# Causal mask of an attention stage: VectorE's minimum with a constant tile in the logits' bank, in place of a TensorE product of mask and identity

## The reference, cut to what matters

```python
for i in range(t // Q_BLOCK):
    z = einsum("bhqd,bhkd->bhqk", q_blk, k[:, :, :ctx]) * scale
    mask = k_pos[None, :] < q_pos[:, None]
    log_1m_beta = where(mask, log_sigmoid(-z), 0.0)
    cs = cumsum(log_1m_beta, axis=3)
    log_a = log_sigmoid(z) + (cs[..., -1:] - cs)
    a = where(mask, exp(log_a), 0.0)
    outs.append(einsum("bhqk,bhkd->bhqd", a, v[:, :, :ctx]))
```

```python
gates = sigmoid(z_g.reshape(bsz, t, N_BRANCH, d) + b_gate[l])
merged = gates[:, :, 0] * y_a + gates[:, :, 1] * y_b + gates[:, :, 2] * y_c
```

## Time and profile before

| | us |
|---|---|
| median of 3 runs | 2188.16 |
| lowest and highest | 2187.33, 2188.7 |
| the profiled execution | 2186.91 |
| its span, first to last instruction | 2185.1 |
| TensorE busy in the span | 2152.9 |
| VectorE, ScalarE, GpSimd busy | 1190.1, 914.4, 920.4 |

### The profile page before, as it was taken

The page is one execution under the profiler, slowest core; times in us unless marked ns, Lnnn a source line. Parts: engine busy times, 40 slices in busy tenths (PEclk is TensorE's granted clock), DMA queues, the critical chain, the costliest instruction groups (busy, mean ns, idle before and its releaser), DMA issues.

```text
span 2185.1 us, 25401 instructions
## 1 busy us (share of the span) xinstructions
PE 2152.9 (99%) x9879; PEld 1778.4 (81%) x9879; DVE 1190.1 (54%) x1778; ACT 914.4 (42%) x1329; POOL 920.4 (42%) x438
## 2 busy tenths in 40 slices
PE   8989999999999999999999999999999999999999
PEld 6868888888888888888888888887777788888887
DVE  6874576444346253566763533888566324765351
ACT  5454444333333333345442323534777334443331
POOL 2423444444443343433444444644432454444443
PEclk9999999999999999999999999999999999999999
DMA  3101222323322222222222234322212232233233
GB/s 133 68 20 54 98 94 97 106 87 102 116 87 82 95 84 82 97 72 94 96 97 97 96 97 148 108 86 69 74 62 68 87 131 95 95 98 105 89 105 97
DMA packets 57656, 200.42 MB, mean 92 GB/s; under 512 B 6400, under 2 KB 7168, under 8 KB 57280
## 3 DMA queue, kind: packets, MB, share of 16 engines
q1 hardware_dynamic: 57536, 198.79, 26.9%
HBM read 194.30 MB, written 4.19 MB: 91 GB/s over the span
## 4 chain that ended last, share of the span: by engine, by line
PE 86%; DVE 6%; issue 3%; ACT 3%; POOL 1%; DMA 0%; SPq 0%; DVEq 0%; ACTq 0%; POOLq 0%
PE ps L321 26%; PE ps L323 26%; PE ps L322 26%; DVE ps L2095 3%; PE ps L349 2%; PE ps L350 2%; PE ps L351 2%; ACT WH L292 1%; PE ps L1229 0%; DMA WS<-in_w 0%; PE ps L364 0%; DVE SC L2243 0%; PE ps L1823 0%; DVE SC L2240 0%; ACT SC L2009 0%
## 5 line engine op out<-in xcount | busy, mean ns | idle before, releaser
L302 POOL TENSOR_TENSOR WL<-WS,WH 128x1024 fp32r<-128x1024 f32 (+2 forms) x362 | 855.7, 2365 | 1139.8 <-ACT WH L292 1139.7
L321 PE MATMUL ps<-H,WH 128*128 128x512 f32 (+1 forms) x1776 | 697.2, 393 | 9.2 <-DVE H L534 9.2
L322 PE MATMUL ps<-H,WH 128*128 128x512 f32 (+1 forms) x1776 | 693.3, 390 | 0.0
L323 PE MATMUL ps<-H,WL 128*128 128x512 f32 (+1 forms) x1776 | 693.2, 390 | 0.0
L292 ACT ACTIVATE WH<-WS 128x1024 fp32r<-128x1024 f32 (+2 forms) x362 | 374.7, 1037 | 451.4 <-PE ps L323 348.9
L321 PEld LDWEIGHTS ps<-H,WH 128*128 128x128 f32 (+1 forms) x1776 | 334.1, 188 | 81.9 <-POOL WL L302 7.1
L323 PEld LDWEIGHTS ps<-H,WL 128*128 128x128 f32 (+1 forms) x1776 | 334.0, 188 | 71.2 <-issue 0.6
L322 PEld LDWEIGHTS ps<-H,WH 128*128 128x128 f32 (+1 forms) x1776 | 334.2, 188 | 67.9 <-issue 0.4
L321 PE MATMUL ps<-G,WH 128*128 128x512 f32 x880 | 342.8, 389 | 0.6 <-DVE G L975 0.6
L322 PE MATMUL ps<-G,WH 128*128 128x512 f32 x880 | 342.4, 389 | 0.0
L323 PE MATMUL ps<-G,WL 128*128 128x512 f32 x880 | 342.4, 389 | 0.0
(11 more groups left out here) (259 smaller groups left out, 2014.8 us busy)
## 6 DMA issues: line engine op xcount, KB each, us to landing
WS<-in_w SPq DMA_DIRECT2D x337, 512.0 KB, 3.2
WS<-in_w SPq DMA_DIRECT2D x24, 384.0 KB, 3.0
X<-in_x SPq DMA_DIRECT2D x8, 256.0 KB, 5.4
xs<-X SPq DMA_DIRECT2D x1, 2048.0 KB, 8.2
X<-xs SPq DMA_DIRECT2D x8, 256.0 KB, 5.9
out<-X SPq DMA_DIRECT2D x8, 256.0 KB, 2.9
X<-in_sg SPq DMA_DIRECT2D x1, 1344.0 KB, 5.5
SC<-in_rot SPq DMA_DIRECT2D x4, 256.0 KB, 3.7
```

The source lines that it names most:

```text
L302: e.tensor_tensor(lo, raw, hi.bitcast(F), ALU.subtract).then_inc(*P.sig("w_lo", i))
L321: e.matmul(out, lh, rh, start=start, stop=False)
L322: e.matmul(out, lh, rl, start=False, stop=False)
L323: return e.matmul(out, ll, rh, start=False, stop=stop)
```

## The change

The constant tile `C_STRICT` becomes an upper bound for the logits: 3e38 where the query is after the key, -1e30 elsewhere (`GONE` is -3e38). TensorE no longer adds the mask; its last logits product raises `az`. VectorE waits for `az` and takes the minimum of the first 128 columns of the bank and the constant tile, in place, for each of the 32 items. The absolute values, on ScalarE for even items and on VectorE for odd ones, wait for this minimum. The two tiles of `CR` and their two copies on ScalarE go. `CR` shrinks from 257 columns to one. The semaphore `row_mm` is merged into `spread`.

```diff
-    c[:, C_STRICT:C_STRICT + 128] = np.where(f < p, 0.0, NEG)
+    c[:, C_STRICT:C_STRICT + 128] = np.where(f > p, -GONE, NEG)
...
-    mean = P.m["CR"][:, 256:257].to_broadcast([128, 128])
+    mean = P.m["CR"][:, 0:1].to_broadcast([128, 128])
...
-    e.matmul(b, mean, lo, start=False, stop=True).then_inc(*P.sig("row_mm", name))
+    e.matmul(b, mean, lo, start=False, stop=True).then_inc(*P.sig("spread", (name, "row")))
...
-        for kl, ql in ((0, 0), (0, 1), (1, 0)):
+        for kl, ql in ((0, 0), (0, 1)):
             for z, kk, qq in heads:
-                e.matmul(z, kk[kl], qq[ql], start=kl + ql == 0, stop=False)
-        for hd, (z, _, _) in enumerate(heads):
-            e.matmul(z[:, 0:128], P.m["CR"][:, 128:256], P.m["CR"][:, 0:128], start=False, stop=True).then_inc(
-                *P.sig("az", n + hd))
+                e.matmul(z, kk[kl], qq[ql], start=ql == 0, stop=False)
+        for hd, (z, kk, qq) in enumerate(heads):
+            e.matmul(z, kk[1], qq[0], start=False, stop=True).then_inc(*P.sig("az", n + hd))
...
             if k % 2 == 0:
                 if k >= 2:
                     e.wait_ge(*P.at("v_lo", k - 2))
-                e.wait_ge(*P.at("az", k))
+                e.wait_ge(*P.at("a_mask", k))
                 e.activation(u, P.ps(("az", k))[:, 0:w], ACT.Abs).then_inc(*P.sig("a_abs", k))
...
             z, u = P.ps(("az", k))[:, 0:w], c_soft(P, hd, kt)
+            e.wait_ge(*P.at("az", k))
+            e.tensor_tensor(z[:, 0:128], z[:, 0:128], P.con(C_STRICT), ALU.min).then_inc(*P.sig("a_mask", k))
             if k % 2:
                 if k >= 2:
                     e.wait_ge(*P.at("v_lo", k - 2))
-                e.wait_ge(*P.at("az", k))
+                e.wait_ge(*P.at("a_mask", k))
                 e.tensor_scalar(u.bitcast(I), z.bitcast(I), 0x7fffffff, None, ALU.bitwise_and).then_inc(
                     *P.sig("a_abs_dve", k))
...
-    for o, s in ((0, C_ID), (128, C_STRICT)):
-        e.activation(P.m["CR"][:, o:o + 128], P.con(s), ACT.Copy).then_inc(*P.sig("cr", o))
```

More of the change, by code:

```diff
@@ L422, in act_row @@
     if biased:
-        e.wait_ge(*P.at("row_mm", name))
+        e.wait_ge(*P.at("spread", (name, "row")))
         e.activation(y, P.ps((name, "row")), ACT.Ln, bias=P.con(C_EPS, 1), scale=-2.0).then_inc(*P.sig("row_act", (name, "ln")))
@@ L2388, in act_program @@
     act_dsa(P, e, "nf0")
-    e.activation(P.m["CR"][:, 256:257], P.con(C_MEAN, 1), ACT.Copy).then_inc(*P.sig("cr", "mean"))
+    e.activation(P.m["CR"][:, 0:1], P.con(C_MEAN, 1), ACT.Copy).then_inc(*P.sig("cr", "mean"))
     act_ffn(P, e, 0, "nf0", "nm1", ("feat", ("aout", 7)), [("p_exp", 31)])
@@ L2491, in program @@
                             ("WS", RING * NXW, F), ("X", 8 * T, F), ("SC", 5888, F), ("TMP", 2 * T, F), ("SQ", 2 * T, F),
-                            ("ACC", T, F), ("CR", 257, R), ("PAR", NPAR, F), ("FP", FPN, F), ("CON", NCON, F),
+                            ("ACC", T, F), ("CR", 1, R), ("PAR", NPAR, F), ("FP", FPN, F), ("CON", NCON, F),
                             ("SM", 508, F)):
```

## The result

The changed kernel takes 2203.36 us, the median of five runs (2202.36 to 2203.9), against 2188.16 for the kernel before in the same series. The ratio is 1.0071 (95% interval 1.006 to 1.0083): 15.2 us slower (13.1 to 18.2 by that interval), where 12.0 were forecast and the range went to 2206. The profiled execution took 2203.9 us, the slowest of the five, with a span of 2202.1, 17.0 more than before.

A forecast was written before the change was run, and what follows sets the result against it. TensorE bounds the program, but in this stage a ScalarE-VectorE chain is about as long; 19.1 us of delay, less 4.0 TensorE gain and 3.1 slack, gives 12.0 us slower: 2200 us, range 2189.5 to 2206.

The forecast's parts named there:

- What bounds the stage: From 1536 to 1706 us, a chain between ScalarE and VectorE is about as long as TensorE's work.
- The price of one minimum: On VectorE, 128 columns with one operand in PSUM: 0.29 us, or 0.33 us in a chain with the hop.
- The bound of 1.69 us from line 2243: Upper end if the minimum stretched beside GpSimd like that line, with both inputs in SBUF: 1.4 us more each time.
- Odd items: VectorE does minimum, then absolute value: chain 0.33 us longer, showing in 14 of 16 items, 4.6 us.
- Even items: ScalarE's absolute value now waits for the minimum in VectorE's in-order queue: 14.5 us of delay in all.
- 3.1 us of slack: Slack before TensorE's use of the splits, eaten in the stage's first six items and taken off the delay.
- TensorE's gain: Dropping 16 pairs of mask products saves 0.25 us a pair, 4.0 us.
- Weights: ScalarE's weight casts come up to 2.5 us later against TensorE, but stay hidden.
- the relief of TensorE would be kept: Rival: VectorE has room for 9.3 us more, TensorE's 4.0 us are gained, 2184.2 us; chance 0.06.
- slack would come back for the items at D: Rival: D items absorb their 2 us wholly, half of the other even items' delay doesn't count; +2, 2190; chance 0.17.
- more VectorE operations are stretched beside GpSimd: Rival: lines 2243 and 2247 stretch more often, 1 to 1.4 us each; five more give 2206; chance 0.09.
- The signs named beforehand: In the later trace: minima 0.28 to 0.30 us, split waits from 12 to over 20, some 15 us more, TensorE's stage share falling.

The follow-up runs named there:

- The early minimum: Changed kernel with each minimum issued one slot earlier on VectorE, ahead of its wait for the previous item's ln: 2186.83 us, ratio 0.9998.
- the two runs: Changed kernel with only odd items masked by minimum, the even by product: 2191.02 us; with only even items by minimum, the odd by product: 2199.25 us.
- the last kernels: Changed kernel with minima and odd absolute values one slot earlier on VectorE: 2182.90 us; the same with the mask products on TensorE as well: 2184.53 us.
- the run with filled gaps: Changed kernel with products by zeros on TensorE ahead of its wait for the split of items 14, 19 and 29: 2201.57 us, ratio 1.0064.

## Why the prediction was right, and where its sum was not

**What bounds the stage** was read rightly: the chain between ScalarE and VectorE. The early minimum shows it, and so does the kernel before with its odd absolute values early: the same work in another order on VectorE, 3.9 us less. The step that follows from it was then not taken to its end, see below.

**The price of one minimum** was 0.29 us taken and 0.293 measured. The bound of 1.69 us from line 2243 didn't come up: 32 minima beside GpSimd, none over 0.300. By the Trainium skill's "SBUF — State Buffer", section "Who interferes with whom", an operation with one input in SBUF outside the two-port modes can't be blocked by GpSimd; the trace agrees, in 32 operations of 0.278 to 0.300 us.

**Odd items**: 4.6 us were the term, 3.8 the measurement, with the odd items' products gone.

**Even items**: 14.5 us were the term, 12.05 the measurement. The term was before slack; 3.1 us of slack were taken off both together. 19.1 - 3.1 = 16.0, and the two runs add up to 15.9. Item 22, forecast 1.66 us late, shows the mechanism: line 2241 starts 2.26 us after the end of the gate multiply, where the walk had 2.20. That the sums agree to 0.1 us is luck in part, since half clock is in the measured one alone.

**TensorE's gain** is the step that failed. The sum took 4.0 us off for the 16 pairs of products. They were worth 0.7 us (no mask against the kernel before), 0.0 to 0.6 (the changed kernel with products against without) and 1.6 (the last kernels). The issue time was right: in the run without a mask the values products of items 0 and 1, with one pair between them, start 0.34 and 0.60 us earlier than in the kernel before, 0.26 us more. But of the 4.0 us there 1.9 became waiting, and some 1.5 (estimated above) went to the clock, which fell behind a wait of 2.47 us. The mistake was to walk the items with TensorE "ahead by 0.75 us until item 4" and then to leave the 4.0 in a sum whose other terms say that TensorE waits for the chain in the end. Where a wait sets TensorE's time, its own savings go into the wait, and a longer wait brought the lower clock. With 0 in place of 4.0 the sum gives 16.0, and 2204; the measured 15.2 to 15.8 lie under it.

**The clock** wasn't in the sum. Some 1 to 2 us of the loss are half clock behind waits, by the run with filled gaps. If sum and measurement agree without it, another term must have been too large by as much, the even items' or the slack's; which, the runs don't tell.

**Weights**: nothing showed there. TensorE had no wait of note for a unit in the stage.

**Rivals.** That the relief of TensorE would be kept is refuted: TensorE is busy for 99% of the span, and 32 instructions less on it brought 0.7 us of 4.0. The Trainium skill's "Perfetto Trace Analysis", section "Identifying the Most-Contended Engine", says to optimize the engine with the highest occupancy first, and to judge TensorE's headroom by, among others, the busy share of its weight loads. That share is 81% here, so TensorE leads either way. But the section ranks engines and gives no price: that the relief is kept was the prediction's step from it. In this stage the trace bears out no gain of that kind; what brought time was VectorE's order (3.9 us). That slack would come back for the items at D is refuted by the even items' 12.05. That more VectorE operations are stretched beside GpSimd isn't seen: line 2244 at 128 columns averaged 0.67 us after and line 2243 0.73 before.

**The signs named beforehand**: minima of 0.28 to 0.30 us, as said. Line 2005's successor starts 0.30 us behind the gate multiply at items 2, 4, 12, 14, 22 and 24, where 0.25 was said. There are over 20 waits (23), but 23.1 us more and not some 15. The rest of the program is unchanged but for 0.5 us ahead of the stage. TensorE's busy share in the stage fell too.

## What to carry to other kernels

An instruction that is moved to another engine can cost more by its place in that engine's queue than by its duration: ask what the other engine's queue holds ahead of it, and which engine's work now waits for that. Here one place cost 16 us and another, in a wait that was there anyway, nothing. And in a stage where the busiest engine waits for a chain, work taken from it can be worth little (0.7 of 4.0 us here); shorten the chain first, and read how much the engine waits in that stage, not its share of the span.

## What the runs showed of the hardware that was not expected

TensorE's granted clock fell from 2.4 to 1.2 GHz three times inside the stage of the changed kernel, for 13.7 us in all. Two of the falls came about 1 us behind waits of 2.29 and 1.77 us, the third within a wait of 4.05 us. Not every such wait brought one: at item 6 the same kernel waited 1.71 us, and the kernel before 1.86 us at item 29, and the clock stayed at 2.4 GHz. Products of 384 columns stood 0.32 us apart in place of 0.17. Filling three gaps with 48 products by zero kept the clock at 2.4 GHz and made the kernel 1.2 to 1.8 us faster: work that computes nothing paid for itself.

The same happened where one wouldn't look for it: in the kernels without a mask and with the early minimum, less work on TensorE made a wait longer (2.47 us in place of 1.86), the clock fell for 3.4 us, and by the estimate above some 1.5 of the 4.0 us saved were gone.
